# A hybrid encoder layer: the mixer's loads and stores are begun by GpSimd's queue instead of the sync queue

## The reference

```python
def layer(l, x, mem_k, mem_v, st):
    h = rmsnorm(x, norm_mix_g[l])
    u = jnp.einsum('btd,dc->btc', h, w_in[l]).astype(f32)
    a_gate, a_x, b_z, b_xbc, b_dt, c_qkv, c_z, c_beta, c_a, d_u = _split_cols(u)
    y_a, lru_h, lru_buf = rglru_mixer(a_gate, a_x, lru_h0, ...)     # linear recurrence, width 256
    y_b, ssd_h, ssd_buf = ssd_mixer(b_z, b_xbc, b_dt, ssd_h0, ...)  # 4 heads, state 128, chunked scan
    y_c, gdn_s, gdn_buf = gdn_mixer(c_qkv, c_z, c_beta, c_a, ...)   # 4 heads, chunked delta rule
    y_d, s5_re, s5_im = s5_mixer(d_u, s5_re0, s5_im0, ...)          # 16 groups of 64 complex states
    x = x + jnp.einsum('btc,cd->btd', jnp.concatenate([y_a, y_b, y_c, y_d], axis=-1), w_out[l])
    x = x + cross_attend(rmsnorm(x, norm_cross_g[l]), mem_k, mem_v, w_cq[l], w_co[l])
    x = x + swiglu(rmsnorm(x, norm_ffn_g[l]), w_ffn_gate[l], w_ffn_up[l], w_ffn_down[l])
```

## Time and profile before

| | |
|---|---|
| time, median of 3 runs | 3783.73 us (3783.28 to 3791.23) |
| the profiled execution | 3785.44 us, of which 3783.7 us is the span of its instructions |
| PE busy | 3475.8 us, 92% |
| DVE, ACT busy | 2149.5 us (57%), 1281.9 us (34%) |
| POOL busy | 91.8 us, 2%, 288 instructions |
| granted clock of TensorE, mean | 0.965 |
| DMA | 786.23 MB, mean 208 GB/s; SP's queue (q1) 742.05 MB, ACT's (q10) 40.25 MB |

### The profile page before, as it was taken

How to read it: one execution, slowest core, us unless ns; L and a number is a source line. 1 busy time by engine, 2 the same in 40 slices (tenths; PEclk the granted TensorE clock), 3 DMA queues, 4 the chain that set the end, 5 groups by cost and what they waited for, 6 DMA issues and landing times.

```text
span 3783.7 us, 61427 instructions
## 1 busy us (share of the span) xinstructions
PE 3475.8 (92%) x23786; PEld 3095.3 (82%) x23786; DVE 2149.5 (57%) x4412; ACT 1281.9 (34%) x2319; POOL 91.8 (2%) x288
## 2 busy tenths in 40 slices
PE   6779889888899988899999999999998999989998
PEld 6767768887689887878888888788887999989998
DVE  6647576647377685565566734554545664644223
ACT  5455243434254444424334323231313331223001
POOL 2210000010000000000000000000000000000000
PEclk9999889999999999999999999999999999999999
DMA  5684556575955548456565674444456565576776
GB/s 202 218 284 162 186 194 211 187 266 186 260 183 182 190 163 304 146 198 210 191 233 216 224 280 148 155 171 162 157 175 240 206 215 199 198 268 225 252 251 213
DMA packets 327938, 786.23 MB, mean 208 GB/s; under 512 B 29792, under 2 KB 147424, under 8 KB 327264
## 3 DMA queue, kind: packets, MB, share of 16 engines
q1 hardware_dynamic: 297376, 742.05, 57.1%
q10 hardware_dynamic: 30272, 40.25, 2.9%
HBM read 607.62 MB, written 174.57 MB: 207 GB/s over the span
## 4 chain that ended last, share of the span: by engine, by line
issue 71%; PE 21%; POOLq 2%; DVE 2%; ACT 1%; DVEq 1%; DMA 1%; ACTq 1%; POOL 0%; SPq 0%
PE banks L505 6%; PE banks L507 6%; PE banks L506 6%; PE banks L1774 1%; ACT whi_sb L986 0%; DVEq L1302 0%; POOLq L2283 0%; POOLq L2281 0%; ACTq L1173 0%; DVE hl_sb L1263 0%; DMA y_t<-x_sb 0%; DMA ldb_sb<-x_t 0%; PE banks L1744 0%; DMA kept_dram<-wlo_sb 0%; DMA wlo_sb<-kept_dram 0%
## 5 line engine op out<-in xcount | busy, mean ns | idle before, releaser
L505 PE MATMUL banks<-hh_sb,whi_sb 128*128 128x384 f32 (+1 forms) x2800 | 1053.2, 376 | 91.0 <-DVE hl_sb L1263 27.4
L506 PE MATMUL banks<-hh_sb,wlo_sb 128*128 128x384 f32 (+1 forms) x2800 | 1020.7, 365 | 0.0
L507 PE MATMUL banks<-hl_sb,whi_sb 128*128 128x384 f32 (+1 forms) x2800 | 1020.3, 364 | 0.0
L505 PEld LDWEIGHTS banks<-hh_sb,whi_sb 128*128 128x128 f32 x2800 | 538.8, 192 | 161.6 <-issue 66.0
L507 PEld LDWEIGHTS banks<-hl_sb,whi_sb 128*128 128x128 f32 x2800 | 537.7, 192 | 49.7
L506 PEld LDWEIGHTS banks<-hh_sb,wlo_sb 128*128 128x128 f32 x2800 | 539.3, 193 | 45.6 <-issue 1.0
L505 PE MATMUL banks<-g_hi_sb,whi_sb 128*128 128x384 f32 (+2 forms) x1264 | 457.3, 362 | 19.7 <-DVE x_sb L1466 9.0
L507 PE MATMUL banks<-g_lo_sb,whi_sb 128*128 128x384 f32 (+2 forms) x1264 | 445.7, 353 | 0.0
L506 PE MATMUL banks<-g_hi_sb,wlo_sb 128*128 128x384 f32 (+2 forms) x1264 | 445.5, 352 | 0.0
L1466 DVE TENSOR_TENSOR x_sb<-x_sb,banks 128x384 f32<-128x384 f32 (+3 forms) x336 | 194.2, 584 | 311.7 <-PE banks L507 291.5
L1244 DVE TENSOR_TENSOR wlo_sb<-raw_sb,whi_sb 128x1024 fp32r<-128x1024 f32 x203 | 248.0, 1225 | 147.7 <-ACT whi_sb L986 143.7
(11 more groups left out here) (449 smaller groups left out, 4716.9 us busy)
## 6 DMA issues: line engine op xcount, KB each, us to landing
whi_sb<-kept_dram SPq DMA_DIRECT2D x392, 512.0 KB, 3.7
wlo_sb<-kept_dram SPq DMA_DIRECT2D x392, 512.0 KB, 4.8
raw_sb<-w SPq DMA_DIRECT2D x176, 512.0 KB, 4.5
kept_dram<-whi_sb SPq DMA_DIRECT2D x112, 512.0 KB, 5.1
kept_dram<-wlo_sb SPq DMA_DIRECT2D x112, 512.0 KB, 5.9
uc_dram<-uc_sb ACTq DMA_DIRECT2D x54, 192.0 KB, 2.9
uc_dram<-uc_sb ACTq DMA_DIRECT2D x36, 256.0 KB, 2.0
plain_sb<-w SPq DMA_DIRECT2D x32, 256.0 KB, 4.9
```

What stands on the lines that cost most here:

```text
L505: eng.matmul(out, xh, yh, start=first, stop=False)
L506: eng.matmul(out, xl, yh, start=False, stop=False)
L507: return eng.matmul(out, xh, yl, start=False, stop=last)
```

## The change

SP's mixer is taken out: SP goes through `sp_section` for all sections, with no mixer pieces between. POOL begins the mixer's transfers, not woven: it runs from one wait to the next. For each pass it waits for `r12_done`, `tok_pe` and `upd` as before, then for the pass's projections in DRAM (`uc_stored`), begins the five loads of the first chunk, and only then works on `scalars(p)` (in pass 0 before the loads). Then the chunks follow in `pool_chunk`, with the same transfers and waits in nearly the same order. The two loads of sample states in pass 0 get a semaphore of their own (`sample_in`), and so do SP's five last stores (`finals_stored`).

```diff
         def pool_mixer(eng):
...
                 if p:
                     eng.wait_ge(tok_pe, p)
                     eng.wait_ge(ms["upd"], PASSES[p - 1][0])
-                scalars(eng, p)
...
-        def sp_chunk(eng, k):
-            c, t0 = k.c, k.c * P
-            more = c + 1 < PASSES[k.p][1]
-            n = 0
-            total = SAMPLE_SECTIONS if k.sample else CHUNK_SECTIONS
-            for n in range(total):
-                if n == 5 and more:
-                    load_q(eng, c + 1)
-                elif n == 9:
-                    k.need("lruy")
-                    eng.dma_start(y_dram[:, 0:2, t0:t0 + P], in_l[:, 2:4, :]).then_inc(ms["y_l"], 16)
-                elif n == 14 and more:
-                    load_l(eng, c + 1)
...
-                yield
-
-        def sp_mixer(eng):
-            for _ in range(N_SETUP):
-                yield
-            for p in range(NP):
                 if p == 0:
-                    eng.wait_ge(setup_inv, 2)
...
+                    scalars(eng, p)
                 for slot in range(UCS):
                     eng.wait_ge(uc_stored[slot], stored(Q_END[p], slot))
                 c = PASSES[p][0]
@@ -2954,12 +2883,71 @@
                 load_l(eng, c)
                 load_x(eng, c)
                 load_z(eng, c)
-                for _ in range(SCALAR_SECTIONS):
-                    yield
-                yield from chunks(eng, p, sp_chunk)
...
+                if p:
+                    scalars(eng, p)
+                else:
+                    eng.wait_ge(setup_inv, 2)
+                    eng.dma_start(s5_xs[:].rearrange("p a b c -> p (a b c)"), t["s5_xs"]).then_inc(sample_in, 16)
+                    eng.dma_start(lru_hs[:].rearrange("p a b -> p (a b)"), t["lru_hs"]).then_inc(sample_in, 16)
+                for c in range(*PASSES[p]):
+                    pool_chunk(eng, Chunk(eng, p, c))
...
+        def pool_chunk(eng, k):
+
+            c, t0 = k.c, k.c * P
+            more = c + 1 < PASSES[k.p][1]
+            if more:
+                load_q(eng, c + 1)
+            k.need("lruy")
+            eng.dma_start(y_dram[:, 0:2, t0:t0 + P], in_l[:, 2:4, :]).then_inc(ms["y_l"], 16)
+            if more:
+                load_l(eng, c + 1)
+            k.need("ych", 1)
+            eng.dma_start(y_dram[:, 2:4, t0:t0 + P], in_x[:, 0:2, :]).then_inc(ms["y_x"], 16)
+            k.need("s5g")
+            eng.dma_start(y_dram[:, 6:8, t0:t0 + P], v3(m["s5t"], 2)).then_inc(ms["y_s"], 16)
+            if more:
+                load_x(eng, c + 1)
+            k.need("ych", 2)
+            eng.dma_start(y_dram[:, 4:6, t0:t0 + P], v3(m["yg"], 2)).then_inc(ms["y_g"], 16)
+            if more:
+                load_z(eng, c + 1)
...
         def _(sp):
             sp.dma_start(par[:], t["par"]).then_inc(par_loaded, 16)
-            weave(sp, sp_section, sp_mixer)
+            for i in range(len(SECS)):
+                sp_section(sp, i)
```

More of the change, by code:

```diff
@@ L697, in program @@
         begun = sem("begun")
+        sample_in, finals_stored = sem("sample_in"), sem("finals_stored")
         states_in, states_out = sem("states_in"), sem("states_out")
@@ L2861, in dve_mixer @@
                 if p == 0:
-                    eng.wait_ge(const_loaded, 16 * 7)
+                    eng.wait_ge(sample_in, 16 * 2)
                 yield from chunks(eng, p, dve_chunk)
@@ L2875, in pool_mixer @@
                     eng.wait_ge(ms["upd"], PASSES[p - 1][0])
-                scalars(eng, p)
+                if p == 0:
+                    scalars(eng, p)
+                for slot in range(UCS):
+                    eng.wait_ge(uc_stored[slot], stored(Q_END[p], slot))
+                c = PASSES[p][0]
+                load_q(eng, c)
+                load_l(eng, c)
+                load_x(eng, c)
+                load_z(eng, c)
+                if p:
[6 more added lines that the diff above has]
+                    pool_chunk(eng, Chunk(eng, p, c))
         def load_q(eng, c):
@@ L2942, in sp_mixer @@
-        def sp_mixer(eng):
-            for _ in range(N_SETUP):
-                yield
-            for p in range(NP):
-                if p == 0:
-                    eng.wait_ge(setup_inv, 2)
[L2948 to L2956, removed]
-                for _ in range(SCALAR_SECTIONS):
-                    yield
-                yield from chunks(eng, p, sp_chunk)
+            if more:
+                load_q(eng, c + 1)
@@ new lines, in pool_chunk @@
+            eng.dma_start(y_dram[:, 4:6, t0:t0 + P], v3(m["yg"], 2)).then_inc(ms["y_g"], 16)
+            if more:
+                load_z(eng, c + 1)
+            if k.sample:
+                k.need("upd")
+                for name, src in (("s_ssd", x_flat[:, 0:2048]), ("s_gdn", x_flat[:, 2048:3072]),
+                                  ("s_s5", s5_xs[:].rearrange("p a b c -> p (a b c)")),
+                                  ("s_lru", lru_hs[:].rearrange("p a b -> p (a b)")),
+                                  ("s_tail", stail[:].rearrange("p a b c -> p (a b c)"))):
+                    eng.dma_start(t[name], src).then_inc(states_out, 16)
@@ L3013, in _ @@
             for name, src in outs:
-                sp.dma_start(t[name], src).then_inc(states_out, 16)
-            sp.wait_ge(states_out, 16 * (5 + len(outs)))
+                sp.dma_start(t[name], src).then_inc(finals_stored, 16)
+            sp.wait_ge(finals_stored, 16 * len(outs))
+            sp.wait_ge(states_out, 16 * 5)
             for stored_pair in out_stored:
```

## The result

The changed kernel takes 3799.79 us (median of 6 runs, 3798.41 to 3804.14), against 3787.09 us for the kernel before in 6 runs of its own: a ratio of 1.0034, 95% interval 1.0024 to 1.0044. The change costs 12.7 us. Its profiled execution took 3799.88 us, of which 3798.1 are the span.

The account below looks back on a forecast made before the run. The prediction took PE, computing 3475.8 of 3783.7 us, as the bound. Its terms, −3.1 for SP's stall and 0 for the rest, took the median 3783.73 to 3781 us, with a range of 3768 to 3801.

Parts of the forecast that it names:

- The prediction's own sign of being wrong: PE idle time changing over 8 us, above all ACT waiting for POOL, or DVE's mean durations rising in the mixer's windows.
- What bounds the kernel, and what SP's stalls cost: PE is the bound; removing SP's 5.1 us stall before the GDN store at 792.77 wins 3.1 us.
- What it moves: the crowd at a pass's start: Five pass-start loads move from 830.16 to about 793, meeting activation loads for `w_out`: 0 us, bounds 0 and +3.
- Sum: Terms −3.1 + 0 + 0 + 0, from the median 3783.73 to 3781 us.
- "0 us" for the wait at 1486: PE's 8.45 us wait before 1486.09 for DVE's residual isn't caused by pass 2's five loads: 0 us, bounds −1 and 0.
- POOL's own time: POOL beginning 174 transfers, at SP's 0.37 to 6.80 us each, stays hidden behind PE's dense work: 0 us.
- The scalars come late: Rival, chance 0.16: five POOL loads taking 67.5 us delay `scalars(p)` for ACT in passes 1 and 3; 3824 at worst.
- POOL and DVE hinder each other: Rival, chance 0.11: 174 POOL transfers slow DVE by 186 us in all, costing PE up to 26; 3807 at worst.
- SP's freedom is worth more: Rival, chance 0.19: all PE waits for weight halves (11.2 us) and cache blocks (5.4) go, giving 3767 us.

Follow-up runs that it names:

- the rolled and the later run: Stores on GpSimd, loads on SP: pass-start loads rolled into the previous pass's last chunk (3785.75 us), or one mixer piece later (3786.35), against the kernel before.

## Why the prediction was wrong

The forecast was 3.1 us less; 12.7 us more were measured. That 3799.79 lies within the stated range of 3768 to 3801 is luck: its upper end stood there for ACT waiting for POOL and for VectorE hindered by POOL, and neither happened. The prediction's own sign of being wrong, PE's idle time changed by more than 8 us, did appear, with 10.9.

- **What bounds the kernel, and what SP's stalls cost: right.** No wait for a transfer of the mixer, before or after. The stall ahead of 792.77 was the place: the waits of 2.60 and 0.50 us are gone in the changed kernel. The term was −3.1; with the GDN store alone moved it measured −3.9, with all four stores −5.5.
- **"What it moves: the crowd at a pass's start" is the step that failed.** It saw that the five loads go from 830 to about 793 and meet the loads for `w_out`, and priced this at 0 us, bounds 0 and +3. It measured +15.3 us, between the run with early pass starts and the run with the chunk loads on GpSimd. Three things were wrong in it. I divided 1.4 MB by the mean rate of the whole span, 208 GB/s, and spread them over 20 us, as if half the bandwidth were free; the windows of that very stretch, which I hadn't read, show the DMA engines at 0.88, and 1.04 at pass 3. I looked at pass 1, and at pass 2's old place, and there are four such places, pass 3's being the worst. And I took the price for the waits alone: after the wait of 5.19 us the granted clock cost another 2.4.
- **Sum.** −4.8 (stores and chunk loads on GpSimd, 3781.15 against 3785.90) and +15.3 make +10.5; measured +12.7, with an interval of 9 to 17 us.
- **"0 us" for the wait at 1486: right as far as it goes.** With the loads gone from that place it is 7.35 us, at 1490.55; all three of its kind make 25.1 us, after 25.2.
- **POOL's own time: 0 us, right, by another way.** It does not spend 0.37 to 6.80 us on a transfer as SP; it begins a big load only when the one before has landed (below). The five took from 801.75 to 826.2 us. I had put 27.5 for it. It begins 160 transfers, not the 174 that the prediction counts; its rival on VectorE would give 171 us with that and not 186.
- **The scalars come late: did not happen.** The loads go one after another, as that rival says, but at 24 us and not 67.5. POOL's first operation of them is at 818.14, its first half ends at 827.2, ACT's table load is at 835.31 in the changed kernel, behind its own work.
- **POOL and DVE hinder each other: no trace of it.** DVE's busy time is 2150.7 against 2149.5 us, and the mean of its splits stays at 1225 ns. The Trainium skill's "SBUF — State Buffer", section "SBUF: two separate sides", has a transfer begun by GpSimd take five times as long beside a VectorE operation in a two-port mode. Here the landing depends on the store: from GpSimd the LRU and SSD stores landed in 2.2 us in the median, against 1.8 and 1.9 from SP, but the S5 store in 3.4 against 1.9 and the GDN store in 5.3 against 1.8. With the GDN store alone on GpSimd it is 6.1 us. VectorE can hardly be the reason: in that run the store begun at 2507.79 landed after 7.02 us, of which VectorE was busy for 0.69. So this case doesn't show that effect, and why these stores land late stays open; it cost nothing in the time.
- **SP's freedom is worth more: no.** 471.9 us of stalls went, and the wait for slots grew by 427.7; the waits of PE for cache blocks (line 894) are 5.3 us after 5.4, and those for weight halves 14.5 after 11.2.

What isn't settled: why a pass start is dearer both before and behind its old place (the rolled and the later run, 5 us each). Part of it may be a stretch near 2900 us. Windows there, for the kernel before:

```profile
2900.00:2910.00 10.00, 8.80 (x64) 8.46 (x65) 1.27 (x3) 3.33 (x11) 0.96 (x5) 1.00 0.52 187
```

and in the changed kernel, where the same work begins:

```profile
2911.00:2921.00 10.00, 8.06 (x30) 8.06 (x31) 0.56 (x1) 0.68 (x4) 1.39 (x7) 0.66 0.33 117
```

The matmuls that stand between 2900 and 2910 in the kernel before take 3.2 us longer here, at a mean granted clock of 0.66 against 1.00, with no longer wait: the one at the start is 2.77 us after 2.80. Of the profiled executions, only that of the kernel before and that with the stores alone moved are without it; in the twelve others, the changed kernel's among them, the matmuls fall behind by 2.7 to 5.0 us between 2882 and 2920, with early pass starts and without, in the run with the chunk loads on GpSimd too, whose median is no worse for it. I count it to no cause.

## What to carry to other kernels

Before a transfer is allowed to start earlier, read what the DMA engines already move in the stretch into which it goes, not the mean of the span, and ask which load in that stretch an engine is about to wait for. Loads with 28 us of room cost nothing that showed at 830 us; begun earlier at the four pass starts, 1.4 MB each time, they cost 15 us, most of it where they met weight halves and raw blocks that PE needed next. An order written by hand that holds a load back can be worth more than the issue time that a second queue saves. What was good in this change is in its stores: they wait for computed results, and out of the queue of the weight loads they gave 5.5 us (0.9985), which beats both kernels.

## What the hardware showed that I had not expected

GpSimd takes 0.56 to 1.08 us to begin one of these loads, against 0.37 to 0.45 on SP where its queue isn't full, and behind a big one it begins the next only when that one has landed: `m_cht_sb`, begun at 231.77, 801.75, 1451.94, 2229.85 and 2842.54 us, landed after 5.26, 7.39, 6.37, 7.35 and 5.25 us, and the next load was begun after 5.58, 7.69, 6.67, 7.65 and 5.55, always 0.3 us behind. Others follow at once: the two `m_in_l_sb` loads (128 and 256 KB) are 0.7 us apart, `m_in_z_sb` (256 KB) stands 0.8 us behind `m_in_x_sb` (384 KB). A limit to what the queue can hold would do this; no run here varied it. GpSimd's own computing can stand behind its transfers, too. Behind the first operation of its scalars the kernel has a `drain`, and the second started only when the last load had landed: at 826.42, 1475.31, 2254.22 and 2861.34 us in passes 1 to 4, each time 0.2 to 0.3 us behind. That is why the first half took 9 us in pass 1, where I had put 2. The same 35.33 MB that were 62208 packets in SP's queue (297376 − 235168, 568 bytes each) are 11072 packets of 3191 bytes in GpSimd's. In the view of the DMA issues of the changed kernel the stores' landings grow along the chunk (count, KB, median us):

```profile
y_dram<-m_in_l_sb POOLq DMA_DIRECT2D x17, 128.0 KB, 2.2
y_dram<-m_in_x_sb POOLq DMA_DIRECT2D x17, 128.0 KB, 2.2
y_dram<-m_ys_sb POOLq DMA_DIRECT2D x17, 128.0 KB, 3.4
y_dram<-m_lb_sb POOLq DMA_DIRECT2D x17, 128.0 KB, 5.3
```

From SP they were 1.8 to 1.9 us. The GDN store, last of the four, is as late with no load on GpSimd at all (5.6), so it isn't the loads in its queue. With only the stores on GpSimd this cost nothing that the time shows.
